# Norm weights turned on TensorE, the first 128 tokens first, and two transfers moved in a decoder layer's queue

## What is computed

```python
z = rmsnorm(h, g_norm) @ w_in          # 2048 x 5656: q, kv, gates, and 3 x 1024 of the short convolution
q, kv, gt, cv = jnp.split(z, SPLITS, axis=-1)
b_gate, c_gate, hc = jnp.split(cv, 3, axis=-1)
conv = b_gate * (conv3(c_gate * hc) + bias)
h = x + rmsnorm_halves(concat(nsa(q, kv, gates, rel_bias), conv), out_gain) @ w_out
h = h + peer_ffn(rmsnorm(h, norm2))     # 16384 single-neuron experts, gathered by row
y = h + sigmoid(rmsnorm(h, norm3) @ w_gate) * (p @ w_ple)
```

## Time and profile before

| | |
|---|---|
| median of the plain runs | 2623.63 us |
| the profiled execution | 2632.44 us |
| its span, first to last instruction | 2630.6 us |
| PE busy | 1712.5 us (65%) |
| DVE busy | 1148.4 us (44%) |
| POOL busy | 905.6 us (34%) |
| ACT busy | 332.0 us (13%) |
| from HBM | 893.70 MB at a mean of 345 GB/s with the writes |

### The profile page before, as it was taken

How to read it: one execution, slowest core, us unless ns; L and a number is a source line. 1 busy time by engine, 2 the same in 40 slices (tenths; PEclk the granted TensorE clock), 3 DMA queues, 4 the chain that set the end, 5 groups by cost and what they waited for, 6 DMA issues and landing times.

```text
span 2630.6 us, 21422 instructions
## 1 busy us (share of the span) xinstructions
PE 1712.5 (65%) x8331; PEld 934.6 (36%) x8331; DVE 1148.4 (44%) x2124; ACT 332.0 (13%) x726; POOL 905.6 (34%) x644
## 2 busy tenths in 40 slices
PE   7599898988898677788678433233233223577677
PEld 3245576487777446533267200000000000122224
DVE  1002112114453764354443466656564775544442
ACT  1000123001000332210110110101101012101002
POOL 0000000003222443322343455665665665655430
PEclk9799896989899676678788666666666665777888
DMA  9683452667999879989999899999999999999996
GB/s 318 209 290 104 141 185 96 223 217 305 396 403 408 322 308 384 361 314 377 376 415 380 355 415 421 421 422 421 422 422 421 421 422 418 396 416 416 415 418 221
DMA packets 228649, 907.12 MB, mean 345 GB/s; under 512 B 29749, under 2 KB 54197, under 8 KB 144614
## 3 DMA queue, kind: packets, MB, share of 16 engines
q0 software_dynamic: 92160, 671.13, 61.9%
q1 hardware_dynamic: 136174, 233.79, 25.5%
q10 hardware_dynamic: 216, 0.86, 0.1%
HBM read 893.70 MB, written 14.52 MB: 345 GB/s over the span
## 4 chain that ended last, share of the span: by engine, by line
DMA 48%; PE 41%; DVE 3%; issue 3%; ACT 2%; POOL 2%; SPq 1%; DVEq 0%; ACTq 0%; PEldq 0%; POOLq 0%
DMA arena<-in_peer_v,arena 30%; PE bank L1668 8%; PE bank L2043 6%; DMA arena<-in_w_in 5%; DMA arena<-in_peer_u,arena 5%; PE bank L2058 5%; DMA arena<-in_peer_wq 3%; PE bank L1732 3%; DMA arena<-in_w_out 2%; PE bank L1860 2%; PE bank L1836 2%; PE bank L1993 2%; PE bank L2163 2%; DMA arena<-in_state_win 2%; PE bank L1973 1%
## 5 line engine op out<-in xcount | busy, mean ns | idle before, releaser
L1465 DVE CUSTOM_DVE_ANT_0 arena<-arena 128x2048 f32<-128x2048 f32 x320 | 731.1, 2292 | 647.3 <-DMA arena<-in_peer_u,arena 643.8
L2043 PE MATMUL bank<-arena 128*32 128x512 f32 x2560 | 461.2, 832 | 661.1 <-DVE arena L1474 501.1
L665 POOL DMA_INDIRECT arena<-in_peer_u,arena x320 | 551.4, 1723 | 879.6 <-DVEq L1444 632.0
L670 POOL DMA_INDIRECT arena<-in_peer_v,arena x320 | 354.0, 1106 | 765.5 <-PE bank L2043 737.3
L2043 PEld LDWEIGHTS bank<-arena 128*32 128x32 f32 x2560 | 69.6, 128 | 1005.9 <-DVE arena L1474 506.8
L1668 PE MATMUL bank<-arena 128*128 128x512 f32 (+2 forms) x544 | 218.3, 562 | 37.4 <-DMA arena<-in_w_in 32.0
L2058 PE MATMUL bank<-arena 128*128 128x192 f32 x1024 | 190.7, 349 | 24.6 <-DMA arena<-in_w_in 23.5
L2058 PEld LDWEIGHTS bank<-arena 128*128 128x128 f32 x1024 | 182.2, 205 | 44.9 <-DMA arena<-in_w_in 29.4
L1668 PEld LDWEIGHTS bank<-arena 128*128 128x128 f32 (+1 forms) x544 | 102.6, 210 | 150.0 <-issue 117.0
L961 ACT ACTIVATE arena<-arena 128x4 f32<-128x4 f32 x80 | 16.8, 211 | 880.0 <-DVE arena L1465 879.8
L2163 PE MATMUL bank<-arena 128*128 128x512 f32 x256 | 117.6, 616 | 0.0
(11 more groups left out here) (245 smaller groups left out, 1532.1 us busy)
## 6 DMA issues: line engine op xcount, KB each, us to landing
arena<-in_w_in SPq DMA_DIRECT2D x22, 2048.0 KB, 13.5
arena<-in_w_in SPq DMA_DIRECT2D x32, 1024.0 KB, 14.8
arena<-in_w_out SPq DMA_DIRECT2D x8, 2048.0 KB, 8.0
arena<-in_peer_wq SPq DMA_DIRECT2D x8, 2048.0 KB, 7.9
arena<-in_w_out SPq DMA_DIRECT2D x16, 1024.0 KB, 14.5
arena<-in_peer_wq SPq DMA_DIRECT2D x16, 1024.0 KB, 23.4
arena<-in_ple_gate SPq DMA_DIRECT2D x32, 512.0 KB, 14.8
arena<-in_ple_gate SPq DMA_DIRECT2D x6, 2048.0 KB, 12.5
```

What stands on the lines that cost most here:

```text
L665: pool.indirect_dma_start(u_row[j], None, I["peer_u"][0], bass.IndirectOffsetOnAxis(idx[:, i, c + j:c + j + 1], 0)).then_inc(u_in[j], 16)
L670: pool.indirect_dma_start(v_row[j], None, I["peer_v"][0], bass.IndirectOffsetOnAxis(idx[:, i, c + j:c + j + 1], 0)).then_inc(v_in[j], 16)
L1465: dve.tensor_tensor_reduce(out=u_row[j], in0=u_row[j], in1=rep_of(i), scale=1.0, scalar=0.0, op0=ALU.mult, op1=ALU.add, accum_out=a4[:, pa ...
L2043: ins = pe.matmul(bank[i % 2][32 * q:32 * q + 32, :], diag[:, k % 2, j, :], v_row[j][:, 512 * q:512 * q + 512], start=(s == 0 and j == 0), ...
```

## The change

Ahead of everything, SP loads the four norm weights as 16 rows of 128 each into `gain_rows`; PE turns them in one transpose to bank 1 and DVE copies them to `gT`. x tile 0 has a semaphore of its own and is issued next, then the weights of block 0, then the rest of x, then `rel_bias`. PE turns tile 0 (16 groups of one 128x128 transpose), makes the bias table, runs blocks 0 and 1, turns tiles 1 and 2 (16 groups of two), and runs blocks 2 to 7. The write of the bias table goes from behind fill 7 to behind the shifts, ahead of fill 18; its read-back from behind fill 11 to behind the `chan_in` loads; the state copy from behind the bias write to behind the stores of the new keys and values; the convolution's weights from ahead of fill 4 to behind fill 7. `pe_in` is loaded earlier, and PE waits for ten evictions instead of twelve ahead of `raw_rows`.

```diff
+    gain_rows = buf(X0, 128)
...
+        for i, name in enumerate(("norm1", "norm2", "norm3", "out_gain")):
+            sp.dma_start(gain_rows[KC * i:KC * i + KC, :], I[name][0].rearrange("(k p) -> k p", p=128)).then_inc(gains_in, 16)
         sp.dma_start(cst, I["cst"]).then_inc(cst_in, 16)
-        tiles_of(xp, xs, h, x_in)
-        sp.dma_start(h[64:128, 2, :], xs).then_inc(x_in, 16)
...
+        sp.dma_start(h[:, 0, :], xp[0]).then_inc(x0_in, 16)
...
-        channel_gain(0, "norm1", first_in)
+        fill_z(0)
+        sp.dma_start(h[:, 1, :], xp[1]).then_inc(x_in, 16)
+        sp.dma_start(h[0:64, 2, :], xs).then_inc(x_in, 16)
+        sp.dma_start(h[64:128, 2, :], xs).then_inc(x_in, 16)
         sp.dma_start(tab[0:NBUCKET, :], I["rel_bias"]).then_inc(first_in, 16)
-        for blk in range(2):
-            fill_z(blk)
-        for i, name in ((1, "norm2"), (2, "norm3"), (3, "out_gain")):
-            channel_gain(i, name, small_in)
+        fill_z(1)
...
+        for blk in range(2, 4):
+            fill_z(blk)
         sp.dma_start(cw[:, 0:3, :], bass.AP(I["conv_w"].tensor, 0, [[0, 128], [CONV, 3], [1, CONV]])).then_inc(cw_in, 16)
...
-        sp.wait_ge(bias_sb, 1)
-        sp.dma_start(bias_dram, rep(bias_row[0:NH, :], [0, 128], [1, NBIAS])).then_inc(bias_out, 16)
-        sp.dma_start(win_s[:, 0:PAST - NT, :], I["state_win"][0].rearrange("b t s g d -> b t (s g d)")[:, NT:, :])\
-          .then_inc(out_done, 16)
...
         sp.wait_ge(u_ready, 1)
         for d, dst in ((1, sh1), (2, sh2)):
             sp.dma_start(dst[d:128, 0, :], cu[0:128 - d, 0, :]).then_inc(shift_a, 16)
+        sp.wait_ge(bias_sb, 1)
+        sp.dma_start(bias_dram, rep(bias_row[0:NH, :], [0, 128], [1, NBIAS])).then_inc(bias_out, 16)
         fill_z(9)
...
+        sp.wait_ge(bias_out, 16)
+        bt = bias_dram.tensor
+        sp.dma_start(bias_p, bass.AP(bt, DMAX - 128, [[NBIAS - 1, 128], [128 * NBIAS, NH], [1, 256]])).then_inc(bias_in, 16)
...
         for b in range(NB):
             sp.dma_start(win_s[b, PAST - NT:PAST, :], z[b * NT:b * NT + NT, 2, 2048:2560]).then_inc(kv_out, 16)
+        sp.dma_start(win_s[:, 0:PAST - NT, :], I["state_win"][0].rearrange("b t s g d -> b t (s g d)")[:, NT:, :])\
+          .then_inc(out_done, 16)
         sp.dma_start(g2[0], bass.AP(I["norm2"].tensor, 0, [[0, 128], [1, D]])).then_inc(g2_in, 16)
...
+        dve.wait_ge(gains_mm, 1)
+        step(dve.tensor_copy(gT.rearrange("p i k -> p (i k)"), bank[1][:, 0:4 * KC]))
+        dve.sem_inc(gains_ev, 1)
...
         pe.wait_ge(cst_in, 16)
-        pe.wait_ge(first_in, 32)
+        pe.wait_ge(gains_in, 64)
+        pe.transpose(bank[1][:, 0:4 * KC], gain_rows[0:4 * KC, :], ident[0:4 * KC, 0:4 * KC]).then_inc(gains_mm, 1)
+        pe.wait_ge(x0_in, 16)
+        transposes(KC, tok_tiles(x_tile, (0,)))
+        pe.wait_ge(first_in, 16)
         pe.wait_ge(dve_step, 2)
...
-        blocks(0, 8, 1)
+        blocks(0, 2, 1)
+        pe.wait_ge(x_in, 48)
+        transposes(KC, tok_tiles(x_tile, (1, 2)))
+        blocks(2, 6, 1)
...
-        pe.wait_ge(mm_ev, 2 + 12)
+        pe.wait_ge(mm_ev, 2 + 10)
         raw_rows(0)
```

More of the change, by code:

```diff
@@ L426, in _ @@
             sp.dma_start(qg_T, I["qk_gain"][0, 0].rearrange("(p o) -> p o", o=1)).then_inc(chan_in, 16)
+        sp.wait_ge(bias_out, 16)
+        bt = bias_dram.tensor
+        sp.dma_start(bias_p, bass.AP(bt, DMAX - 128, [[NBIAS - 1, 128], [128 * NBIAS, NH], [1, 256]])).then_inc(bias_in, 16)
+        for r in range(2 * NH):
+            sp.dma_start(bias_s[NT * r:NT * r + NT, :],
+                         bass.AP(bt, (r % NH) * 128 * NBIAS + DMAX - PAST, [[NBIAS - 1, NT], [1, DMAX + 1]])).then_inc(bias_in, 16)
         for blk in range(10, 12):
@@ L447, in compress_weights @@
               .then_inc(w1_in[part], 16)
-        sp.wait_ge(small_in, 16 * 5)
+        sp.wait_ge(small_in, 16 * 2)
         sp.wait_ge(mm_done, 11)
@@ L455, in _ @@
         sp.wait_ge(mm_done, 12)
+        for kind in range(2):
+            sp.dma_start(pe_in[kind][0:BLK, :], I["cmp_pe"][0, kind]).then_inc(pe_in_s, 16)
         compress_weights(0, 1)
@@ L458, in _ @@
             sp.dma_start(w2[kind], I["cmp_w2"][0, kind].rearrange("(a p) h -> p a h", p=128)).then_inc(w2_in, 16)
-            sp.dma_start(pe_in[kind][0:BLK, :], I["cmp_pe"][0, kind]).then_inc(pe_in_s, 16)
         for b in range(NB):
-            sp.wait_ge(t_mm, KC + 1 + b + 1)
+            sp.wait_ge(t_mm, 2 * KC + 1 + b + 1)
             page_rows(1, b)
@@ L481, in fill_rows @@
             fill(2 * n + half, w_view[name][:, 8 * half:8 * half + 8, 512 * blk:512 * blk + 512])
-        sp.wait_ge(t_mm, KC + 2 * (NB + 2))
+        sp.wait_ge(t_mm, 2 * KC + 2 * (NB + 2))
         fill_rows(N_OUT, 0, "out")
-        sp.wait_ge(t_mm, KC + 2 * (NB + 2) + 12)
+        sp.wait_ge(t_mm, 2 * KC + 2 * (NB + 2) + 12)
         sp.wait_ge(kv_out, 16 * (5 + NB))
@@ L691, in odd_transposes @@
             tcount[0] += n
-        act.wait_ge(first_in, 32)
-        odd_transposes(KC, lambda e, c: e.activation(xT[:, c, 0:TOK], bank[7][:, 0:TOK], ACT.Copy, scale=gT[:, 0, c:c + 1]))
+        act.wait_ge(gains_ev, 1)
+        odd_transposes(KC, lambda e, c: e.activation(xT[:, c, 0:128], bank[7][:, 0:128], ACT.Copy, scale=gT[:, 0, c:c + 1]))
         root(stats[:, 0:3], stats[:, 3:6])
@@ L713, in _ @@
         for part, region in enumerate((bg, cu, sh1)):
+            if part == 1:
+                odd_transposes(KC, lambda e, c: e.activation(xT[:, c, 128:TOK], bank[7][:, 128:TOK], ACT.Copy, scale=gT[:, 0, c:c + 1]))
             for j in range(2):
@@ L1131, in _ @@
         step(dve.memset(tab[NBUCKET:NBUCKET + 1, :], NEG))
[L1132 to L1136, removed]
+        dve.wait_ge(gains_mm, 1)
+        step(dve.tensor_copy(gT.rearrange("p i k -> p (i k)"), bank[1][:, 0:4 * KC]))
+        dve.sem_inc(gains_ev, 1)
+        even_transposes(KC, lambda e, c: e.tensor_scalar(xT[:, c, 0:128], bank[6][:, 0:128], gT[:, 0, c:c + 1], None, ALU.mult))
+        dve.wait_ge(x0_in, 16)
+        dve.wait_ge(x_in, 48)
         for t in range(3):
@@ L1141, in _ @@
         dve.sem_inc(n1_ready, 1)
+        dve.wait_ge(bias_mm, 1)
+        dve.tensor_copy(bias_row[0:NH, :], bank[2][0:NH, 0:NBIAS]).then_inc(bias_sb, 1)
+        even_transposes(KC, lambda e, c: e.tensor_scalar(xT[:, c, 128:TOK], bank[6][:, 128:TOK], gT[:, 0, c:c + 1], None, ALU.mult))
         dve.wait_ge(mm_ev, 2 + 6)
@@ L1162, in _ @@
         ins.then_inc(xn_ready, 1)
-        dve.wait_ge(small_in, 16 * 5)
+        dve.wait_ge(small_in, 16 * 2)
         dve.wait_ge(mm_ev, 2 + 12)
@@ L1354, in item @@
                 if blk == 0:
-                    dve.wait_ge(x_in, 112)
+                    dve.wait_ge(x_in, 96)
                 dve.wait_ge(rb_used, 4 * blk + 4)
@@ L1644, in transposes, with tok_tiles, x_tile @@
                 evs[par] += 1
-        def tok_tiles(src, rows=ROWS):
-            return lambda c: [(128 * t, src(t, c)[0:rows[t], :], rows[t]) for t in range(3)]
+        def tok_tiles(src, tiles=(0, 1, 2)):
+            return lambda c: [(128 * t, src(t, c)[0:ROWS[t], :], ROWS[t]) for t in tiles]
+        def x_tile(t, c):
+            return h[:, t, 128 * c:128 * c + 128]
         pe.wait_ge(cst_in, 16)
-        pe.wait_ge(first_in, 32)
+        pe.wait_ge(gains_in, 64)
[3 more added lines that the diff above has]
+        pe.wait_ge(first_in, 16)
         pe.wait_ge(dve_step, 2)
-        pe.matmul(bank[0][0:NH, 0:NBIAS], tab[0:NBUCKET + 1, :], cst[0:NBUCKET + 1, C_OH:C_OH + NBIAS],
+        pe.matmul(bank[2][0:NH, 0:NBIAS], tab[0:NBUCKET + 1, :], cst[0:NBUCKET + 1, C_OH:C_OH + NBIAS],
                   start=True, stop=True).then_inc(bias_mm, 1)
-        pe.wait_ge(x_in, 64)
-        transposes(KC, tok_tiles(lambda t, c: h[:, t, 128 * c:128 * c + 128]))
         pe.wait_ge(t_ev[0], 8)
         pe.wait_ge(t_ev[1], 8)
-        pe.wait_ge(bias_sb, 1)
         def product(done, f, par, tiles, width=512):
@@ L1690, in root_rows @@
                              start=True, stop=True)
-        blocks(0, 8, 1)
+        blocks(0, 2, 1)
+        pe.wait_ge(x_in, 48)
+        transposes(KC, tok_tiles(x_tile, (1, 2)))
+        blocks(2, 6, 1)
+        pe.wait_ge(t_ev[0], 16)
+        pe.wait_ge(t_ev[1], 16)
+        pe.wait_ge(bias_sb, 1)
         blocks(8, 2, 2)
```

19 lines of the change are left out of this document (3 added, 16 removed).

## The result

The changed kernel takes 2615.97 us (median of 20 runs, 2608.96 to 2629.73). The kernel before, run 20 times beside it, takes 2633.59 (2619.38 to 2636.98). The ratio is 0.9943, 95% interval 0.993 to 0.9956: about 15 us less by the ratio, 17.6 by the medians. The forecast was 26.6 less, and 2597 on a scale that rested on three runs of before. The profiled execution took 2611.32 us around a span of 2609.5, that is 21.1 less than the profile of before.

A forecast was written before the change was run, and what follows sets the result against it. PE's path bounds, with 31.97 us lost at block 4 behind bias write and state copy. -24.7 + 0 - 1.9 = -26.6 on 2632.4 gives 2605.8, 2597 on the median's scale; own range 2590 to 2604, wide 2588 to 2618.

The forecast's parts named there:

- rival (a): Block 9: the engine with shift 1 does its share of the bias write late; wait 16.2 + 2.1, 2615; chance 0.22.
- the rest up to the late products: After block 9, to the samples' input products: shorter waits at `raw_rows` and `cmp_pe`, -1.9, bounds -3 and +4.
- I take the low end, 0: Block 9: bias write runs from T8 for 28 us, fill 18 lands at T8 + 33.3, before T8 + 35.4; no wait.
- The start: Up to block 2: block 0 at 30.3, 4.0 earlier; second transposes 10.7, slow beginnings; block 2 at 71.5.
- (b): Start: small table `rel_bias` not held behind the fills, block 0 at about 21, -36, 2588; chance 0.06.
- (c): State copy fills the 49 us from 71 to 120; PE waits 20 for `v_prompt` at the attention, 2617; chance 0.07.
- (d): Block 9: the bias write alone needs 49 us, fill 18 lands at T8 + 72.6, wait 37.2 + 2.1, 2636; chance 0.05.

The follow-up runs named there:

- run 20: No label, but part of "run 20 times": the kernel before, unchanged, run 20 times beside the changed kernel; median 2633.59 us.

## Why the prediction was right or wrong

It was right in direction and on the 31.97 us in front of block 4. It was too large by half (26.6 against 17.6 by the medians, 15 by the ratio), as it had the wait at block 9 at nothing. The 2616 us lie between the wide bounds of 2588 and 2618, taken to cover rival (a), and outside the forecast's own 2590 to 2604. Step by step, predicted against the first profile:

| step | predicted | measured |
|---|---|---|
| block 0 starts | 30.3 | 29.41 |
| blocks 0 and 1 end | 60.8 | 59.5 |
| block 2 starts | 71.5 | 69.83 |
| wait before block 4 | 0 | 0.81, the usual gap |
| block 8 starts (T8) | 160.9 | 159.48 |
| the write's packets | T8 to T8 + 28 | T8 + 2.5 to T8 + 37.6 |
| fill 18 lands | T8 + 33.3 (bounds to T8 + 51.6) | T8 + 43.6 |
| wait and slow beginning at block 9 | 0 (0 to 18.3) | 8.3 + 2.0 |
| state copy ahead of `v_prompt` | hidden | hidden, 387.69 against 397.15 |
| the rest up to the late products | -1.9 | -5.4 and +1.6 in two pairs of profiles |

**The step that failed: "I take the low end, 0".** The low end was T8 + 33.3: the write begins at T8, takes 28 us, and fill 18 lands 5.3 behind it. Measured was T8 + 43.6, which is 2.5 + 35.1 + 6.0. All three terms were too small. The write began behind shift 2. Its length was mis-sized even without a late engine: 29.9 us in the kernel before, where its own rows held the warning, as 1.60 MB at the 49 GB/s shown make 32.7 and not 28. (The stretch from 72 to 100 us is not flat either: from 82 to 90 fills run beside the write, with 118 to 241 GB/s. The forecast needed only its end.) And in the changed kernel one engine was late by shift 1, which landed at T8 + 14.9, 12.4 us after the others had begun: 4.4 us more by the run with cut shifts. By the same run the shifts on few engines also account for 6.4 us of the write's late beginning.

The argument for 0, 49 GB/s is twice 25, had a part right: with seven engines writing beside the shift the stretch shows 75 less some 26, and with eight still 49, so an eighth engine adds nothing. That the late one finds the limit free when the others finish also fits: 49 of the 1024 packets fell behind 194 us and took 3.1 us, 25 GB/s, the rate of one engine alone. (That it was one engine is read from the rate; the trace names none.) But it finds it free only then, so it can't finish with them. The Trainium skill's rule (DMA: Bandwidth & Descriptors, section Why a DMA increments its semaphore by 16 and not by 1), that 127 rows use one engine and it is among the eight of a transfer with 8 rows, pointed there; the 35.1 us with whole shifts against 30.7 with cut ones agree with it. The Trainium skill's port map (SBUF — State Buffer, section Door 1: The DMA port swizzle (why `[64,N]` ≈ `[32,N]`)) gives 27.2 GB/s for each of the two ports; the trace has 49 to 50 GB/s, about 24.6 for each, with seven engines as with eight.

Rival (a) named the late engine and the right place, at 18.3 us instead of 10.3; it had 0.22. It had the late engine need 28 us for its eighth from the shift's landing on; it needed 22.7 (T8 + 14.9 to T8 + 37.6).

**The scale.** I took 8.8 us off because three runs of before had a median of 2623.63 below the profiled 2632.44. Twenty runs give 2633.59: the profile was typical and the three runs were low. With 10.0 put back and 10.3 for block 9, 2597 becomes 2617, against 2616; that they meet so closely is partly luck, as the rest up to the late products came out at -5.4 in one pair of profiles and +1.6 in the other. A profile and a median of three that disagree by 0.3% don't say which is off.

**The start.** The terms were near (block 0 within 0.9 us), and the sum for it, 4.0 gained and about 13 spent on the second transposes and slow beginnings, was in the prediction; what I didn't draw out is that the start is a loss: 101.11 against 95.36 with the old one. The 10.12 us for the 1 KB table were predicted (28.3 against 28.0), and the load one place behind `cst` takes them back.

**The rivals.** (b), the small table passes the fills: no. (c), the copy fills the 49 us: no, the write alone leaves 14.01 at block 4. (d), a write of 49 us: no, it took 29.4 to 35.4 in these profiles. The forecast of 31.97 gone, with both pieces named, held: 14.01 and 2.77 are left when one is moved. The state copy is 8 rows of 126,976 words, the 4.06 MB of the prediction, and not of 63,488 words as said ahead of it.

## What to carry to other kernels

When a transfer is moved in a queue, ask which DMA engines it uses and what those hold at the new place, not how many bytes it has: a copy of 127 partitions (one engine) ahead of a write of eight rows cost 10.3 us, and cutting 127 into 112 and 15, or letting the next weights go first, took them back. Take a transfer's time from its packets, first to last, and hold it against bytes by rate: here 28 us stood for 30, and 2 us of margin were none. Put small loads that gate an engine at the head of the queue: 1 KB in line behind two 2 MB fills and the rest of x cost 10 us. And try the parts of a change alone; here the queue gave all of the gain and the new start took some of it away, until the small load was moved too.

## What was not expected

- The granted clock fell to 0.50 in the middle of the second transposes (0.50 in the stretch from 66 to 68 us, with PE in short bursts), not only where PE stood. The pairs of transposes stretched from 1.05 to 1.40 us, and block 2 took 16.10 for 13.97. DVE's timeline:

```profile
62.71 0.42 DVE L1142 TENSOR_SCALAR arena<-bank,arena 128x192 f32<-128x192 f32 x1 [0.63 <-PE bank L1642]
...
67.84 0.42 DVE L1142 TENSOR_SCALAR arena<-bank,arena 128x192 f32<-128x192 f32 x1 [0.98 <-PE bank L1642]
```

- Block 4 bore about 16 us of foreign work in the queue without a wait: the copy's 19.2 us left 2.77, the write's 30.1 left 14.01.
- Eight engines on the write moved no more than seven did: 49 to 50 GB/s.
